# Where one matrix memory's sample products stand among the prompt's score blocks: a new order on two engines in the second mixer's heads

## The reference, cut to what matters

```python
qk  = einsum(q, k) * exp(dlog - m_row)          # scores, decayed, causal
num = einsum(qk, v)
den = maximum(abs(sum(qk)), exp(-m_row))
h   = num / den
C_new = einsum(k * ws, v)                        # the prompt's new state, 512 x 512 a head
y = (head_norm(h) * g + skip * xc) * silu(z)
```

## Time and profile before

| what | value |
|---|---|
| median of 3 runs | 2513.46 us (2510.49 to 2513.63) |
| the profiled execution | 2514.56 us |
| its span, first to last instruction | 2512.8 us |
| PE busy, share of the span | 2423.3 us, 96% |
| DVE, ACT, POOL busy | 1342.2, 797.9, 365.9 us |
| granted TensorE clock, mean | 0.984 |
| heads 0, 1, 2, 3 of the second mixer | 59.84, 64.50, 62.18, 62.44 us |

### The profile page before, as it was taken

The page is one execution under the profiler, slowest core; times in us unless marked ns, Lnnn a source line. Parts: engine busy times, 40 slices in busy tenths (PEclk is TensorE's granted clock), DMA queues, the critical chain, the costliest instruction groups (busy, mean ns, idle before and its releaser), DMA issues.

```text
span 2512.8 us, 44459 instructions
## 1 busy us (share of the span) xinstructions
PE 2423.3 (96%) x18881; PEld 2302.1 (92%) x18881; DVE 1342.2 (53%) x1772; ACT 797.9 (32%) x1105; POOL 365.9 (15%) x494
## 2 busy tenths in 40 slices
PE   6999999999979999999999999998999989999999
PEld 6999999999869999999999999988655579999998
DVE  4333434577565444434434445833588776666654
ACT  3222223444323222222222223233444433222222
POOL 1000000222001214000000000000122113445432
PEclk9999999999889999999999999999999999999999
DMA  3333334232204555332333332321444446889974
GB/s 110 89 88 90 103 92 131 83 86 73 67 23 127 159 163 134 98 92 83 89 90 92 109 91 71 92 72 48 147 144 151 154 141 200 296 294 298 297 243 165
DMA packets 444571, 325.19 MB, mean 129 GB/s; under 512 B 14714, under 2 KB 391846, under 8 KB 444302
## 3 DMA queue, kind: packets, MB, share of 16 engines
q1 hardware_dynamic: 427512, 274.90, 37.1%
q0 software_dynamic: 13232, 42.10, 4.7%
q10 hardware_dynamic: 3728, 6.87, 0.8%
HBM read 278.95 MB, written 44.99 MB: 129 GB/s over the span
## 4 chain that ended last, share of the span: by engine, by line
PE 84%; DVE 9%; ACT 2%; DMA 2%; issue 2%; POOL 0%; SPq 0%; DVEq 0%; POOLq 0%; ACTq 0%
PE ps L1943 72%; PE ps L2421 3%; DMA m_c_ring<-in_state_mlstm_C 2%; PE ps L2209 2%; DVE m_qcs L1707 1%; PE ps L2046 1%; PE ps L2349 1%; DVE m_acc L1707 1%; DVE m_w_lo L1196 1%; PE ps L2007 0%; ACT m_w_hi L704 0%; PE ps L2336 0%; PE ps L2105 0%; DVE m_tmp L1719 0%; DVE m_rstd L1211 0%
## 5 line engine op out<-in xcount | busy, mean ns | idle before, releaser
L1943 PE MATMUL ps<-m_n_hi,m_w_hi 128*128 128x260 f32 x3808 | 774.7, 285 | 13.2 <-DVE m_w_lo L1196 11.6
L1943 PE MATMUL ps<-m_n_hi,m_w_lo 128*128 128x260 f32 x3808 | 770.3, 284 | 0.0
L1943 PE MATMUL ps<-m_n_lo,m_w_hi 128*128 128x260 f32 x3808 | 769.2, 284 | 0.0
L1943 PEld LDWEIGHTS ps<-m_n_hi,m_w_hi 128*128 128x128 f32 x3808 | 591.4, 190 | 16.7 <-DVE m_w_lo L1196 8.9
L1196 DVE TENSOR_TENSOR m_w_lo<-m_w_raw,m_w_hi 128x1024 fp32r<-128x1024 f32 (+1 forms) x312 | 408.2, 1308 | 363.9 <-ACT m_w_hi L704 359.3
L1943 PEld LDWEIGHTS ps<-m_n_hi,m_w_lo 128*128 128x128 f32 x3808 | 590.3, 189 | 0.0
L1943 PEld LDWEIGHTS ps<-m_n_lo,m_w_hi 128*128 128x128 f32 x3808 | 589.5, 189 | 0.0
L704 ACT ACTIVATE m_w_hi<-m_w_raw 128x1024 fp32r<-128x1024 f32 (+1 forms) x312 | 347.9, 1115 | 234.0 <-PE ps L1943 228.0
L1943 PE MATMUL ps<-m_h_hi,m_w_hi 128*128 128x260 f32 x1408 | 283.8, 283 | 0.0
L1943 PE MATMUL ps<-m_h_hi,m_w_lo 128*128 128x260 f32 x1408 | 283.1, 282 | 0.0
L1943 PE MATMUL ps<-m_h_lo,m_w_hi 128*128 128x260 f32 x1408 | 282.5, 282 | 0.0
(11 more groups left out here) (432 smaller groups left out, 2550.3 us busy)
## 6 DMA issues: line engine op xcount, KB each, us to landing
m_w_raw<-in_ffn_w_gate SPq DMA_DIRECT2D x88, 512.0 KB, 3.9
m_w_raw<-in_ffn_w_up SPq DMA_DIRECT2D x88, 512.0 KB, 3.8
m_w_raw<-in_ffn_w_down SPq DMA_DIRECT2D x64, 704.0 KB, 4.6
m_c_ring<-in_state_mlstm_C SPq DMA_DIRECT2D x128, 256.0 KB, 3.4
m_u_ring<-in_state_mlstm_C SPq DMA_DIRECT2D x128, 256.0 KB, 6.1
out_C_s<-m_u_ring POOLq DMA_DIRECT2D x128, 256.0 KB, 5.4
m_w_raw<-in_ev_w_in SPq DMA_DIRECT2D x32, 512.0 KB, 4.0
m_w_raw<-in_ml_w_in SPq DMA_DIRECT2D x32, 512.0 KB, 4.0
```

The source lines that it names most:

```text
L1943: last = mm(out[:, t, :], w[:, j % 2, c], r[:, k0 + k, t * HT:(t + 1) * HT], start=start and k == 0 and n == 0, stop=stop and k == kt - 1 ...
```

## The change

The change reorders instructions on ACT and DVE in every head; PE, GpSimd and SP keep their order, and no instruction is added or taken away.

On DVE, `sample_center`, `sample_divisor` and `samples(h, 0)` come right behind `weigh(h, 1)`; `samples(h, 1)` comes behind `weigh(h, 2)`, `samples(h, 2)` behind `weigh(h, 3)`. From head 1 on `y_full(4p + 2)` stands between samples 0 and `weigh(h, 2)`, `y_full(4p + 3)` between samples 1 and `weigh(h, 3)`, and the two last `y_low` on either side of samples 2.

On ACT, `sample_rows` and `first_product(h, 0)` come behind the exponentials of block 1; `y_high(4p + 2)`, `first_product(h, 1)` and `sample_square` behind those of block 2; `y_high(4p + 3)` behind those of block 3, and then `new_state(h, 0)`, `sample_root` and `new_state(h, 1)`.

```diff
--- before.py
+++ after.py
@@ -1104,14 +1104,19 @@
                     if h and c == 0:
                         y_high(4 * p)
                         y_high(4 * p + 1)
-                    elif h and c < 3:
-                        y_high(4 * p + c + 1)
-                if h:
-                    sample_rows(p)
-                    sample_square(p)
-                first_product(h, 0)
+                    if c == 1:
+                        if h:
+                            sample_rows(p)
+                        first_product(h, 0)
+                    if c == 2:
+                        if h:
+                            y_high(4 * p + 2)
+                        first_product(h, 1)
+                        if h:
+                            sample_square(p)
+                if h:
+                    y_high(4 * p + 3)
                 new_state(h, 0)
-                first_product(h, 1)
                 if h:
                     sample_root(p)
                 new_state(h, 1)
@@ -1821,28 +1826,28 @@
                     y_low(4 * p)
                 weigh(h, 0)
                 if h:
-                    y_full(4 * p + 2)
                     y_low(4 * p + 1)
                 weigh(h, 1)
-                if h:
-                    y_full(4 * p + 3)
-                    y_low(4 * p + 2)
-                weigh(h, 2)
-                if h:
-                    y_low(4 * p + 3)
-                weigh(h, 3)
                 if h:
                     sample_center(p)
                 sample_divisor(h)
                 samples(h, 0)
                 if h:
+                    y_full(4 * p + 2)
+                weigh(h, 2)
+                samples(h, 1)
+                if h:
                     sample_variance(p)
-                samples(h, 1)
+                    y_full(4 * p + 3)
+                weigh(h, 3)
                 if h:
                     sample_scale(p)
+                    y_low(4 * p + 2)
+                samples(h, 2)
+                if h:
+                    y_low(4 * p + 3)
                 dve.wait_ge(*reach("o_tke", 5 * h + 4))
                 link(v.tensor_scalar(vsum[:, :], vsum[:, :], -1.0 / DH, None, ALU.mult))
-                samples(h, 2)
                 samples(h, 3)
                 dve.wait_ge(*reach("o_c", 4 * (h + 1)))
                 for c in range(NC):
```

More of the change, by code:

```diff
@@ L1838, in _ @@
                 if h:
-                    sample_variance(p)
+                    y_full(4 * p + 2)
+                weigh(h, 2)
                 samples(h, 1)
                 if h:
+                    sample_variance(p)
+                    y_full(4 * p + 3)
+                weigh(h, 3)
+                if h:
                     sample_scale(p)
+                    y_low(4 * p + 2)
+                samples(h, 2)
+                if h:
+                    y_low(4 * p + 3)
                 dve.wait_ge(*reach("o_tke", 5 * h + 4))
                 link(v.tensor_scalar(vsum[:, :], vsum[:, :], -1.0 / DH, None, ALU.mult))
-                samples(h, 2)
                 samples(h, 3)
```

## The result

The changed kernel takes 2524.47 us (median of 5 runs, 2521.09 to 2528.9) against 2513.63 (5 runs): the ratio is 1.0043, interval 1.0031 to 1.0054, 10.8 us slower. The forecast was 2515.9 with a range up to 2522.0, and its likeliest outcome, a difference within 0.2%, did not come. The profiled execution is the fastest of the five, 2521.09 us, span 2519.3; the stretch before the heads happens to end 4.1 us earlier in it than in the profile of before (first product of head 0 at 1750.66 and 1754.72).

The account below looks back on a forecast made before the run. PE, 84% of the chain that ended last, was taken to bound the kernel; heads 0 to 3 at -2.0, +1.2, +2.25 and +1.0 summed to +2.45 on a median of 2513.46: 2515.9 us, range 2509.5 to 2522.

Parts of the forecast that it names:

- likeliest outcome: Whole kernel: a time within 0.2% of the kernel before, given a chance of 0.65.
- The mechanism up to `state(2)`: Heads 1 to 3: ACT's copy of `state(0)` comes late, so PE newly waits some 5 us at `state(2)`.
- signs of being wrong: No wait at `state(2)`; clock 1.00 with samples 3 early; or clock 0.50 in all three heads and the tail equally late.
- The clock: PE's granted clock after the new wait at `state(2)`: a cost taken as 0 to 1.0 us a head.
- About 1 us of it hides: Of the clock's cost at `state(2)`, about 1 us hides because PE's own path is 1.1 ahead of DVE's.
- PE's own path: Head 1, `state(2)` to the gathering on PE: numerators could start at 1869.2, 1.1 us later than before.
- The slack: Head 1: DVE's samples 3 and centring start the numerators 2.1 us later; PE's path, 1.1 later, has room beside it.
- The tail: After head 3: PE's 6.18 us wait takes half of the 0 to 2.1 delay, leaving +1.0.
- Head 0: First head: earlier samples remove PE's waits of 1.30 and 0.55, -2.0 us in all; 0 if transfers hold samples 3.
- The centring: DVE's centring of `m_vtok` between samples 3 and the numerators, taken as 1.65 us.
- The rival "slower": Clock falls at each new wait, head 3's delay reaches the end, head 0 gains nothing: +7.2, 2520.7; chance 0.24.

Follow-up runs that it names:

- e3_product_first: The changed kernel with ACT's `first_product(h, 3)` put in front of `new_state(h, 2)`; ratio 1.0039 to the kernel before.
- e6_late_sum: The changed kernel with GpSimd's `key_sum` released by the centring's end instead of the last state; ratio 1.0031 to the kernel before.
- e5_order: The changed kernel, ACT's first products, `sample_square`, root and `new_state(h, 0)` moved earlier, DVE's `sample_variance` in front of samples 1; ratio 0.9973 to the kernel before.
- e11_before_sum: The kernel before, with only `key_sum` released by the centring's end instead of the last state; ratio 0.9995 to the kernel before.
- e9_order_sum: The changed kernel with ACT's and DVE's order untied and `key_sum` released by the centring's end as well; ratio 0.9959 to the kernel before.
- e2_copy_first: The changed kernel with ACT's `new_state(h, 0)` put in front of `y_high(4p+3)`; ratio 1.0021 to the kernel before.

## Why the prediction was wrong

The mechanism up to `state(2)` was right: the last score block waits for nothing, `y_high` holds the copy of `state(0)`, `state(2)` waits 5.23 us in head 1 (5.2 was said), `sample_scale` 2.87 (about 3), the wait in front of the gathering is gone. `state(2)` starts 4.36, 4.28 and 3.65 us later after the head's first product (3.9 was said). What fell is the step from there to the sum: the price of the clock, the path of samples 3 beside PE's, and what the tail absorbs. The last of the prediction's signs of being wrong came true: the granted clock fell to 0.50 in all three heads, and the tail was as late as the numerators.

- **The clock.** Taken as 0 to 1.0 a head, measured 1.66, 2.93 and 2.07 (states 2 and 3 less their 7.13): 6.7 us in sum, and 6.0 and 6.9 with the same three waits in e3_product_first and e6_late_sum. "About 1 us of it hides" failed with it. PE's own path was said to come out 1.1 later than before: 3.9 less the old waits of 2.27 and 0.55. With the measured numbers of head 2 it is 4.28 + 2.93, less old waits of 3.18 (2.63 and 0.55 in its trace), plus the 0.82 that remain: 4.85, and the numerators started 4.78 later. The same sum gives 4.03 in head 1 (measured 3.94) and 4.27 in head 3 (4.20). In head 1 the numerators' own 1.4 came back as forecast (8.90 us instead of 10.32), so that the head grew by 2.53 only. The rule from the page "TensorE: Matmul & The Clock Gate" of the Trainium skill, section "HAM oscillation", which the prediction set against head 2 of the kernel before, is what the trace of after shows: the clock is at 0.50 behind the wait in every one of the three heads.
- **The slack.** DVE's samples 3 were followed as a path beside PE's. They are not beside it: ACT's `first_product(h, 3)` stands behind the copy of `state(2)`, so a late `state(2)` makes samples 3 late. The run that takes this knot out (e3_product_first) shortens the wait in front of the numerators by 2.6 us over the four heads.
- **The tail.** Half of head 3's delay was to vanish in PE's 6.18 us wait. That wait is there unchanged, and its row starts 12.18 us after the first output product in both traces (2003.68 to 2015.86, 2010.37 to 2022.55): what ends it begins with head 3's numerators too, which start 22.6 and 22.3 us before that row. From the row to the end of the span it is 497 us in both. Head 3 counted 3.92, not 1.0.
- **Head 0.** Taken as -2.0 from the earlier trace rows (the 0.15 in it for the semaphore's way stands in no row), measured -0.48; with head 0's old code it comes out at 59.38 in another execution. Its samples 3 stood behind the same knot: without it the heads' row has 58.52, and with the late `key_sum` 57.70.
- **The centring** was taken as 1.65; beside `key_sum` it took 2.68, and 4.87 where all of it fell there.

By heads, predicted -2.0, +1.2, +2.25, +1.0; measured -0.48, +2.53, +4.78, +3.92: 8.3 us too little, 1.5 of it head 0, 3.9 the two middle heads, 2.9 the tail. The rival "slower" named the right case, the clock at each new wait and head 3's delay reaching the end, with 0.24; its 7.2 us were still too little, since it was made with the same 1.0 us a head for the clock.

## What to carry to other kernels

A wait that moves onto the matmul engine can cost the slow clock behind it on top of its length, and before calling any part hidden, follow what the other engine's instructions stand behind in its own program order: here the "independent" samples hung on the very product that came late. With the transfers started early, the kernel became faster than before (6.8 us) only once the copies that free PSUM and the first products stood in front of whatever waits for the other engine. A long wait near the end absorbs a delay only if what ends it doesn't begin with the delayed work.

## What the hardware showed that was not expected

Beside GpSimd's addition some of VectorE's operations stop whole, however small: 128x4 values took 2.34 us instead of 0.16 beside an addition of 2.35 (e5_order), and four centring operations took 4.87 instead of 1.67 beside both additions of `key_sum` (e3_product_first). That agrees with the rule of the Trainium skill's page "SBUF — State Buffer", section "Who interferes with whom", that the two engines' shared port pair is locked for a whole instruction and not divided. Others do not stop: in e11_before_sum a reciprocal of 128x512 values ran beside the same two additions in 3.35 us, as long as it takes with no addition beside it (timelines of GpSimd and VectorE in head 0):

```profile
1803.62 2.37 POOL L644 TENSOR_TENSOR m_k_tok<-m_k_tok 128x1024 f32<-128x1024 f32 x1 [25.00 <-DVE m_m_vtok L1849]
...
1804.72 3.35 DVE L1856 RECIPROCAL m_tmp<-m_tmp 128x512 f32<-128x512 f32 x1
```

Moving `key_sum` put it beside other operations, and part of the loss moved with it: in e9_order_sum it stood on one 128x32 operation (2.24 us instead of 0.19).

The clock's price was not the same for like waits. In e2_copy_first `state(3)` stood 2.38, 2.00 and 1.69 us in the three heads; behind the second it took 5.40 us at a granted clock of 0.68, behind the other two 3.70 at 1.00. TensorE's timeline in head 2:

```profile
1924.02 5.40 PE L2371 MATMUL ps<-m_m_vtok,m_k_tok 128*128 128x512 f32 x8 [2.00 <-ACT m_st_c L1050]
```

Why one of three like waits cost 1.7 us and the others nothing, no run here shows.
